# Hybrid block and HGRN2 block on one core: the heads' sum of squares as two rounded products, with the low part made by GpSimd and the product three projection rows later

## The reference, cut to what matters

```python
def _rms_norm(x, g):
    return x * lax.rsqrt(jnp.mean(x * x, -1, keepdims=True) + RMS_EPS) * g
...
    o = (o_intra + jnp.moveaxis(o_inter, 0, 1)).reshape(bsz, seq, HG_HEADS, HG_DV)
    o = _rms_norm(o, o_g.astype(f32).reshape(HG_HEADS, HG_DV)).reshape(bsz, seq, HG_WIDTH)
    o = o * jax.nn.silu(g_raw.astype(f32))
```

## Time and profile before

| | |
|---|---|
| median of three runs | 2945.0 us |
| the profiled execution's own time | 2946.08 us |
| its span | 2944.3 us |
| TensorE busy | 2914.4 us (99%) |
| VectorE busy | 1995.8 us (68%) |
| ScalarE busy | 1466.8 us (50%) |
| GpSimd busy | 1463.4 us (50%) |
| granted TensorE clock, mean | 0.998 of full speed |
| stage of the heads, head 0 to head 7 | about 2015 to 2242 us from the span's start |

### The profile page before, as it was taken

The page is one execution under the profiler, slowest core; times in us unless marked ns, Lnnn a source line. Parts: engine busy times, 40 slices in busy tenths (PEclk is TensorE's granted clock), DMA queues, the critical chain, the costliest instruction groups (busy, mean ns, idle before and its releaser), DMA issues.

```text
span 2944.3 us, 46687 instructions
## 1 busy us (share of the span) xinstructions
PE 2914.4 (99%) x16304; PEld 2491.7 (85%) x16304; DVE 1995.8 (68%) x3186; ACT 1466.8 (50%) x2518; POOL 1463.4 (50%) x1108
## 2 busy tenths in 40 slices
PE   8999999999999999999999999999999999999998
PEld 6888888878898888888887889988888898798997
DVE  7985686876674598577697667557775563773645
ACT  4243333485474424333346737636565573564645
POOL 5433443555566454443445555643434375555745
PEclk9999999999999999999999999999999999999999
DMA  4222222211333332322221123332223334333322
GB/s 154 94 78 71 90 81 82 85 50 64 108 103 131 115 107 72 93 78 71 86 93 58 44 94 122 122 108 79 80 70 129 94 101 134 97 121 99 110 93 86
DMA packets 75090, 276.01 MB, mean 94 GB/s; under 512 B 8224, under 2 KB 9120, under 8 KB 74144
## 3 DMA queue, kind: packets, MB, share of 16 engines
q1 hardware_dynamic: 70560, 254.84, 27.0%
q10 hardware_dynamic: 4352, 18.81, 1.7%
HBM read 266.27 MB, written 7.34 MB: 93 GB/s over the span
## 4 chain that ended last, share of the span: by engine, by line
PE 91%; issue 3%; POOL 2%; DVE 2%; ACT 1%; DVEq 0%; DMA 0%; ACTq 0%; POOLq 0%; SPq 0%
PE gem L784 13%; PE gem L786 13%; PE gem L785 13%; PE xp L876 4%; PE xp L878 4%; PE xp L877 4%; PE xp L1413 2%; PE xp L1415 2%; PE xp L1414 2%; PE gem L1268 2%; PE gem L1270 2%; PE gem L1269 2%; PE gem L964 2%; PE gem L966 2%; PE gem L965 2%
## 5 line engine op out<-in xcount | busy, mean ns | idle before, releaser
L621 POOL TENSOR_TENSOR wlo<-raw,whi 128x512 fp32r<-128x512 f32 x676 | 922.4, 1387 | 1148.3 <-ACT whi L1498 1148.0
L1498 ACT ACTIVATE whi<-raw 128x1024 fp32r<-128x1024 f32 x338 | 356.6, 1056 | 362.7 <-PE gem L786 226.7
L784 PE MATMUL gem<-hhi,whi 128*128 128x512 f32 x1184 | 461.4, 390 | 0.0
L786 PE MATMUL gem<-hhi,wlo 128*128 128x512 f32 x1184 | 461.2, 390 | 0.0
L785 PE MATMUL gem<-hlo,whi 128*128 128x512 f32 x1120 | 435.9, 389 | 0.0
L786 PEld LDWEIGHTS gem<-hhi,wlo 128*128 128x128 f32 x1184 | 222.3, 188 | 46.7
L784 PEld LDWEIGHTS gem<-hhi,whi 128*128 128x128 f32 x1184 | 222.2, 188 | 46.5
L784 PE MATMUL gem<-zhi,whi 128*128 128x512 f32 x656 | 256.7, 391 | 0.0
L786 PE MATMUL gem<-zhi,wlo 128*128 128x512 f32 x656 | 255.8, 390 | 0.0
L785 PEld LDWEIGHTS gem<-hlo,whi 128*128 128x128 f32 x1120 | 210.2, 188 | 43.9
L785 PE MATMUL gem<-zlo,whi 128*128 128x512 f32 x528 | 205.5, 389 | 0.0
(11 more groups left out here) (525 smaller groups left out, 8140.0 us busy)
## 6 DMA issues: line engine op xcount, KB each, us to landing
raw<-in_slabs SPq DMA_DIRECT2D x410, 512.0 KB, 3.5
U<-in_slabs SPq DMA_DIRECT2D x32, 512.0 KB, 3.8
tab<-in_slabs SPq DMA_DIRECT2D x18, 512.0 KB, 3.5
z_low<-in_slabs SPq DMA_DIRECT2D x12, 512.0 KB, 4.1
z_plain<-in_slabs SPq DMA_DIRECT2D x6, 512.0 KB, 4.1
U<-in_x SPq DMA_DIRECT2D x4, 512.0 KB, 6.2
U<-in_x ACTq DMA_DIRECT2D x1, 2048.0 KB, 8.2
xsave<-U ACTq DMA_DIRECT2D x1, 2048.0 KB, 7.0
```

The costliest lines, as they stand in the source:

```text
L621: part = pool.tensor_tensor(wlo[:, k % 4, c], raw[:, k % 2, c], whi[:, k % 4, c].bitcast(f32), O.subtract)
L784: pe.matmul(o, wh, hi, start=(n == 0), stop=False)
L786: mm = pe.matmul(o, wl, hi, start=False, stop=(n == len(terms) - 1))
L1498: act.activation(whi[:, k % 4, :], raw[:, k % 2, :], A.Copy).then_inc(hi_done, 1)
```

## The change

The square of `OH` is written twice by ScalarE: rounded into `OSQ_HI` (a further tile of the work area) and in full into `OSQ`. GpSimd waits for `hg_osq`, subtracts, and writes the rounded difference over `OSQ` (as `OSQ_LO`). This stands in GpSimd's order behind the fourth slab of the group of `head_products(p)`, so ahead of the first slab of the next group. TensorE makes two products of rounded operands with `ones_r` in place of one product of full precision with `ones`; it waits for the subtraction and no longer for ScalarE. The semaphore is one that exists, `yr_clear`, which stands at `2 * DEPTH` by then. The row before which the sum stands is three later for all heads.

```diff
+        OSQ_HI, OSQ_LO = (Ur[:, n * T:(n + 1) * T] for n in (25, 23))
...
+        hg_low, CLEARED = yr_clear, 2 * DEPTH
...
-            lows(at, RUN_STARTS[DEPTH])
+            at_heads = (BLOCK_G + HG[0] + 1) * 4
+
+            def head_low(p):
+
+                pool.wait_ge(hg_osq, p + 1)
+                pool.tensor_tensor(OSQ_LO, OSQ, OSQ_HI.bitcast(f32), O.subtract).then_inc(hg_low, 1)
+
+            lows(at, at_heads)
+            with pool.Fori(0, 8) as p:
+                G = p + at_heads // 4
+                for k in range(4):
+                    low(G, k)
+                    if k == 3:
+                        head_low(p)
+            lows(at_heads + 32, RUN_STARTS[DEPTH])
...
-                pe.wait_ge(hg_osq, p + 1)
-                pe.matmul(xp[:, 2, :], ones[:, :], OSQ, start=True, stop=True).then_inc(hg_var, 1)
+                pe.wait_ge(hg_low, CLEARED + p + 1)
+                pe.matmul(xp[:, 2, :], ones_r[:, :], OSQ_HI, start=True, stop=False)
+                pe.matmul(xp[:, 2, :], ones_r[:, :], OSQ_LO, start=False, stop=True).then_inc(hg_var, 1)
                 rows(cuts[4], 32)
 
-            head_products(0, BLOCK_G + 1, BLOCK_U + 1, (14, 16, 18, 23, 27))
-            head_products(1, BLOCK_G + 2, BLOCK_U + 2, (0, 11, 15, 19, 24))
-            head_products(2, BLOCK_G + 3, BLOCK_U + 3, (0, 9, 13, 17, 22))
+            head_products(0, BLOCK_G + 1, BLOCK_U + 1, (14, 16, 18, 23, 30))
+            head_products(1, BLOCK_G + 2, BLOCK_U + 2, (0, 11, 15, 19, 27))
+            head_products(2, BLOCK_G + 3, BLOCK_U + 3, (0, 9, 13, 17, 25))
             with pe.Fori(3, 7) as p:
-                head_products(p, BLOCK_G + 1 + p, BLOCK_U + 1 + p, (0, 6, 11, 15, 20))
+                head_products(p, BLOCK_G + 1 + p, BLOCK_U + 1 + p, (0, 6, 11, 15, 23))
             Gv, uv = BLOCK_G + GM_V[0], BLOCK_U + GM_V[1]
-            head_products(7, Gv, uv, (0, 6, 11, 15, 23))
+            head_products(7, Gv, uv, (0, 6, 11, 15, 26))
...
                 act.activation(OH, xp[:, 3, :], A.Copy)
                 act.drain()
+                act.activation(OSQ_HI, OH, A.Square)
                 act.activation(OSQ, OH, A.Square).then_inc(hg_osq, 1)
                 act.wait_ge(hg_var, p + 1)
```

## The result

The changed kernel takes 2953.24 us (median of nine runs, 2952.2 to 2955.12) against 2945.03 us for the kernel before: +8.2 us, ratio 1.0028 with a 95% interval of 1.002 to 1.0036. The prediction was 2949.1 us, +4.1, with a range of 2944.5 to 2954; the time lies within the range, near its upper end, and the loss is twice the forecast.

The account below looks back on a forecast made before the run. TensorE, busy 99% with 91% of the chain, was taken as the bound; waits at the scores of heads 1 to 7, less the product's saving, gave +4.1 us, so 2949.1 us against the median, range 2944.5 to 2954.

Parts of the forecast that it names:

- The product: TensorE, each head: two rounded products take 0.47 us instead of 0.87, saving 0.40 a head, 3.2 us over eight.
- The second square and the subtraction at no cost: Heads: ScalarE's extra square, at most 0.63 us, lies beside TensorE's rows; GpSimd's subtraction ends 0.1 us in time; cost nothing.
- rival (3): TensorE's wait for `hg_low`: subtraction 0.6 us too late per head, 4.8 more, +8.9 in all, 2953.9 us; chance 0.16.
- Where TensorE waits: At the scores, for VectorE's `el_q`: starts move +1.47, +0.84, +1.47 at heads 1 to 3, +0.18 each at heads 4 to 7.
- I take 1.47, between them: VectorE's chain from norm to `el_q`: `lev_ready` taken as 1.47 us later, a value between 1.38 and 1.67.
- The step before it: ScalarE's logarithm starts 1.67 us later: 2.06 for three rows, plus 0.67, less the old 1.06.
- the two bounds: Delay of `el_q`: 1.67 us if GpSimd gets the turn before VectorE's split (sum +5.5), 1.38 if VectorE does (+3.5).
- a hand-over of 0.04 us: ScalarE's exponential to VectorE's norm: 0.04 us allowed for the hand-over, so 0.20 of the 1.67 us delay is hidden.
- the 2948.4 us: Sum stated for the skill's rule that the first issuer locks the shared ports for a whole instruction, so the lower bound holds.
- Nothing later gives it back: Behind the heads, TensorE's few waits hang on work that itself follows TensorE, so the +4.1 us loss stays.
- the forecast's own range: Whole kernel: 2948 to 2951.5 us around the forecast of 2949.1, the forecast having chance 0.63.
- a price of the waits that the trace before doesn't show: TensorE's waits: 0.09 of the forecast's 0.63 allowed for their cost taking the loss over 5.9 us.

Follow-up runs that it names:

- the rows alone: The kernel before with only the sum of squares moved three rows later, old full-precision product kept and nothing new on GpSimd; 2953.17 us, 1.0031.
- the slab first: The changed kernel with GpSimd's subtraction for the head placed behind the next group's first slab instead of ahead of it; 2953.37 us, 1.0028.

## Why the prediction was half right

*The product.* 0.87 us before and 0.47 after, 3.2 us over eight heads: right, and shown alone (-3.0 in the stretch, -2.8 in the median).

*The second square and the subtraction at no cost.* Right, and the working nearly to the tenth. Timelines of GpSimd and VectorE at head 4:

```profile
2151.22 1.71 POOL L729 TENSOR_TENSOR Ur<-U,Ur 128x512 fp32r<-128x512 f32 x1 [12.51 <-ACT U L2167]
```

```profile
2151.09 0.69 DVE L3242 TENSOR_TENSOR U<-U 128x512 f32<-128x512 f32 x1
2155.44 0.75 DVE L3305 SCALAR_TENSOR_TENSOR U<-U,vec 128x512 f32<-128x512 f32 x1 [3.65 <-ACT U L1535]
```

VectorE's third long instruction of `k_levels` began at 2151.09, 0.13 us ahead of GpSimd, which needed 1.71 us and ended at 2152.93. TensorE's load for the product of 2153.24 stands 0.23 ahead of it, at 2153.01: a reserve of 0.1 us, as forecast, and rival (3), the subtraction too late, didn't happen. One row earlier it happens: the load is 0.7 us late in heads 3 to 6 there.

*Where TensorE waits.* Right: at the scores, for VectorE, in all seven places, 1.9, 1.2, 1.9 and four times 0.5 us; and VectorE idle ahead of the norm (3.65 us). The idle times of the loads, which the prediction named as the sign, came out longer than its 1.5 to 2 and 0.5 to 0.8: 2.3, 1.6 and 2.3 us at heads 1 to 3, and 0.95.

*How long.* Here the term "I take 1.47, between them" was too small. The step before it was right: the logarithm 1.67 us later. But of the two bounds the upper one held, and what was mis-sized is the hand-over from ScalarE to VectorE. Timelines at head 4: the exponential, then GpSimd and VectorE behind it.

```profile
2154.66 0.63 ACT L1535 ACTIVATE U<-U 128x512 f32<-128x512 f32 x1
```

```profile
2157.75 1.29 POOL L624 TENSOR_TENSOR wlo<-raw,whi 128x512 fp32r<-128x512 f32 x1 [2.32 <-ACT whi L1516]
```

```profile
2157.79 1.79 DVE L2452 TENSOR_TENSOR hlo<-U,hhi 128x512 f32 x1
2159.51 1.77 DVE L3261 TENSOR_TENSOR U<-U 128x512 f32<-128x512 f32 x1
...
2163.17 2.28 DVE L3242 TENSOR_TENSOR U<-U 128x512 f32<-128x512 f32 x2 [0.19 <-issue]
```

The exponential ends at 2155.29, and VectorE takes up the norm at 2155.44. I had reckoned with a hand-over of 0.04 us in place of the 0.24 of before, so with VectorE 0.20 us sooner behind the exponential and its split 0.05 us ahead of GpSimd's subtraction. But the hand-over took 0.14 to 0.15 us in heads 0 to 6, though VectorE was idle, and 0.03 in head 7 alone. So VectorE gained only 0.10, and its split was 0.04 us behind: 2157.79 against 2157.75. The split took 1.79 us, and `el_q` ended at 2165.45, 10.16 us after the exponential, as before (2129.65 - 2119.49): the 0.10 us was lost again at the first turn.

So the delay was 1.67, for which the prediction had +5.5; the second trace of the changed kernel, without a fall of the clock in the heads, has +5.2 in the stretch and +5.5 in its time. The terms agree one by one. By the starts of the corners it is +1.62, +1.05 and +1.63 for heads 1 to 3, 0.32 to 0.36 for each of heads 4 to 7, and -0.45 behind head 7; with 1.67 the prediction's terms are 1.67, 1.04, 1.67, 0.38 and -0.40.

By the Trainium skill (SBUF — State Buffer, Who interferes with whom) contention is for the pair of ports that VectorE and GpSimd share, and the one that issues first keeps it for the whole instruction; the page says the latter of VectorE's modes with two ports, and of a `tensor_tensor` from SBUF that it contends with GpSimd's reads. The trace agrees for these instructions: 1.79 us for a split that came 0.04 us later. In head 7 of the same trace the split comes 0.33 us ahead of GpSimd's subtraction (2247.55) and takes its 0.69 us:

```profile
2247.22 0.69 DVE L2452 TENSOR_TENSOR hlo<-U,hhi 128x512 fp32r<-128x512 f32 x1
```

What was wrong was who is first, and with it the 2948.4 us that I had hung on that rule. In heads 0 to 6 GpSimd is first in every kernel here, so no run shows the lower bound, 1.38.

*What was not in the sum at all.* The clock. In the changed kernel's first trace one fall behind a wait adds 1.5 us to the stretch, +6.7 instead of +5.2. The nine runs of 2952.2 to 2955.1 us lie about one, two or three such steps above the single one of 2950.45, and the mean granted clock of an execution goes the same way: 0.998 in that one, 0.997 in the seven up to 2953.6, 0.996 in the two near 2955. So the median's +8.2 would be 5.2 and two further falls. That part is argued: one of the nine has a trace here, and it shows one fall in the heads and one behind them. Of the waits of 1.8 us or more in the heads' traces (two each in the changed kernel, its second trace, the rows alone and the slab first), three of eight were followed by a fall; of the waits of 1.6 us and less in the heads, none. Outside the heads it was 11 of 13 for the wait of 2.3 us, and near the start falls stood by waits of 1.5 us in three traces. I had priced a wait of TensorE at its length. What decides whether a fall comes stays open.

*The range.* That 2953.24 lies in the stated range is luck. The upper end, 2954, was set by rival (3), the late subtraction, which did not happen; the forecast's own range, 2948 to 2951.5, holds the traced execution with no fall in the heads (2950.45) and not the median.

*Nothing later gives it back.* Right: the differences outside the stretch are those of the falls there.

*Chances.* Slower by over 0.2% had 0.26 and came true, but not by the slower rival, the subtraction (0.16). It came by a price of the waits that the trace before doesn't show, for which the text held 0.09.

## What to carry to other kernels

When an instruction is moved later in the queue of the engine that sets the time, follow its result around the loop to the next wait of that engine and write the reserve down for every turn of the loop; here it was 0, 0.5, 0 and 1.2 us against a delay of 1.7. If there is none, move the consumer as well: three rows for the sum with two or three for the scores turned +8 us into -2.3. And where two engines race for a turn by less than 0.1 us, take the bad end into the sum and not the middle; read the hand-over where the waiting engine is idle, and at the same place in the loop.

## What the runs showed of the hardware that I had not expected

A wait of TensorE of about 1.9 us can be followed, some 0.4 to 1 us after it ends, by some 3 us at half the granted clock (0.50, so 1.2 GHz), which costs 1.5 us more, and in other executions of the same kernel it is not. Such falls, here or elsewhere in the kernel, are the likely cause of the steps of 1 to 1.6 us between executions of one kernel: the time outside the stretch goes by their number in all 13 traces.

VectorE's instruction of 0.69 us took 1.79 us because GpSimd was 0.04 us ahead. And in the changed kernel a hand-over from ScalarE to an idle VectorE took 0.14 us in seven heads and 0.03 in the eighth; why they differ, no run shows.
